# Weight sums ahead of two output DMAs, a router's table from one-hots in parts, and the choices' weights on GpSimd: one step of a hybrid decoder layer

## The chip, the core and the metric

One core of a Trainium2 chip runs the whole program: TensorE (matmuls, PE), VectorE (DVE), ScalarE (ACT), GpSimd (POOL) and SyncE (SP, which only issues DMAs here), each with its own queue of instructions, and 16 DMA engines. The metric is the device time of one execution in microseconds (us), the median of several runs. Lower is better.

## What is computed

One decoder layer on 1024 prompt tokens and on 8 sequences of 4 new tokens, 1056 rows in all, of width 1024, in float32. Cut to what matters:

```python
h    = rmsnorm(x, norm_mix)
proj = h @ w_in                          # 1024 -> N_IN columns, split among three token mixers
#  A gated DeltaNet (4 heads x 128, short conv on q/k/v, chunks)
#  B chunked causal spatial gating (4 groups x 64)     C RWKV-7 (4 heads x 64)
x    = x + concat(o_a, o_b, o_c) @ w_out
# hierarchical MoE
h    = rmsnorm(x, norm_ffn)
gsel = argmax(gl)                        # 1 of 4 groups, gl = h @ router_group_w + b
gw   = softmax(gl)[gsel]
top_v, top_i = top_k(el[gsel], 2)        # 2 of the group's 4 experts
tw   = softmax(top_v) * gw               # weights of the two choices
x    = x + sum_e gate[e] * ((silu(h @ w_gate[e]) * (h @ w_up[e])) @ w_down[e])
y    = rmsnorm(x, norm_final)
```

The new recurrent states, the last convolution rows and the last normalised row of each sequence (`shift_prompt`, `shift_sample`) are outputs too.

## The kernel before

All order is written by hand: each engine has one program, and the engines meet through semaphores (`wait_ge`, `then_inc`). A wait holds up all that stands behind it in the same engine's program.

**The projection.** Activations lie transposed in `hT`. The first 14 column blocks of `w_in` (v, the q/k/v blocks of mixer A) are taken two blocks at a time, a *pair*, by a Strassen-like scheme of seven half-size products (`seven_products(p, ch)`, matmuls at L553) in place of eight: for each pair p (0 to 6) and each half of the tokens, ch = 0 or 1, the products M1, M6, M2, M7, M4, M5, M3 follow one another, each eight matmuls and a bit under 1.8 us. M1, M2, M4, M3 and others use four sums and differences of the pair's weight halves, t1 to t4, or the halves themselves. GpSimd makes these sums in `weight_sums(p)` (L463 to L468): four subtractions of 128 x 512, with two drains. It waits for the pair's weights (`w_in`, loaded by SyncE in `load_pair(p)`) and, from p = 2 on, for the last product of pair p-2 (`s.prod`), which frees the buffers of the sums. TensorE waits for `s.sums_w >= p+1` before the first product of a pair. VectorE adds the products into the outputs (`halves`, L1089 to L1100), and does the short convolution of each finished block in between (L1107 to L1119); the products rotate through six PSUM banks, so a product waits for the add of the product six places before it.

GpSimd's program in this stretch is: sums of pair 0, sums of pair 1, a small mask product (L473), then a wait for `s.shc >= 2` and two DMAs with the last normalised rows (L475, L476), then sums of pairs 2 and 3, a wait and a DMA (L480), sums of pairs 4 to 6. `s.shc` counts two copies by VectorE (L1028) of rows that TensorE transposed in `last_tokens(0)` and `last_tokens(1)` (L583); the second of these stands behind all products of pair 1.

**The router's table.** At the end of the output projection each token has two choices c = 0, 1 of an expert. Tokens lie in TILES = 9 tiles of up to 128; each choice gets a place, a *slot* of 32 rows (`sk`) and a row in it (`fl`), by a chain of small steps on VectorE (`step` is one operation and a drain, so all of these steps have line 2786). Then for each choice two one-hots are made: `Arow` (L2870, 18 x 32 elements per partition) of the row, `Bcol` (L2875, 9 x 104 per choice) of the slot. `Arow` times `behind` gives the half of `Aid` that carries row numbers (GpSimd, L2251), `Arow` times the choice's weight `route.w` the half that carries weights (VectorE, L2874). 18 matmuls (L2534) of `Aid` by `Bcol`, 9 for each choice, sum up the table; it is turned by one more step (L2537, L2538) into lists of rows and of weights by slot. The five steps that make `route.w` from the exponentials stand in the middle of VectorE's chain, between the first slots of the experts and the ranks:

```python
dve.wait_ge(s.ex, 2)
step(dve.tensor_reduce, den[:], route.exps[:, :, 0:NG], AX_X, ALU.add)
step(dve.scalar_tensor_tensor, den[:], route.exps[:, :, NG], 1.0, den[:], ALU.add, ALU.mult)
step(dve.reciprocal, route.w[:, 0], den[:])
step(dve.tensor_tensor, route.w[:, 1], route.exps[:, :, NG], route.w[:, 0], ALU.mult)
step(dve.tensor_scalar, route.w[:, :, NT], route.w[:, :, NT], route.valid[:], None, ALU.mult)
```

**The experts.** With the table known, GpSimd gathers the rows of a slot by indirect DMAs (L3018), and TensorE works through some 76 slots (L3086, L3097), while SyncE loads the experts' weights. Expert 0's weights are asked for as soon as the output projection is over.

## Time and profile before

| what | value |
|---|---|
| median of 3 runs | 1267.41 us (1266.54 to 1269.93) |
| the profiled execution's own time | 1270.75 us |
| its span in the trace | 1269.0 us |
| TensorE busy (matmuls) | 1188.6 us, 94% |
| VectorE, ScalarE, GpSimd busy | 518.8, 339.5, 560.3 us |
| mean granted TensorE clock | 0.97 |

The trace is of one execution; every number in the rows below is from it, in us from the start of its span unless marked ns. A line number is one of the kernel before. Idle time of an engine costs only where something that ends late waits for that engine, so the rows are to be read for who waited for whom, and in which order.

### The profile page before, as it was taken

Reading aid. Unit: us, or ns where it says so; the run is one execution under the profiler, and the core shown is the slowest. Engines: PE = TensorE matmul, PEld = TensorE weight load, DVE = VectorE, ACT = ScalarE, POOL = GpSimd, SP = SyncE. Lnnn points to the kernel's source line nnn. Section 1 sums busy time; section 2 is a strip of 40 time slices with the busy share of each in tenths; the row PEclk is TensorE's granted clock in tenths of the full one; section 3 lists DMA queues with packets and bytes.
Section 4 is the critical chain, followed back from the end, with each engine's and each line's share of the span. In section 5 each row is a group of like instructions: output and inputs, shape, how many; then the busy total and the mean of one; then the engine's idle time right before and its main releaser. Section 6 shows DMA issues by size and latency. Waiting matters only on the chain. (4 is left out here: it accounts for less than half of the span.)

```text
span 1269.0 us, 31522 instructions
## 1 busy us (share of the span) xinstructions
PE 1188.6 (94%) x12736; PEld 849.9 (67%) x12736; DVE 518.8 (41%) x1252; ACT 339.5 (27%) x787; POOL 560.3 (44%) x818
## 2 busy tenths in 40 slices
PE   9996999999999999999998999959999999999990
PEld 7785888856666667778764554447777777777760
DVE  3453887755285524564532113252222222222223
ACT  5002003253342145456432132211111111111114
POOL 7403111020650236878732021026666666666662
PEclk9998999999999999999998999969999999999995
DMA  6301120114303100000084313189999897898838
GB/s 208 100 1 34 35 67 18 32 60 137 63 21 92 50 17 15 17 23 16 11 243 159 101 67 113 45 303 381 308 373 338 270 374 247 289 374 288 266 51 290
DMA packets 139882, 187.12 MB, mean 147 GB/s; under 512 B 37272, under 2 KB 85903, under 8 KB 139786
## 3 DMA queue, kind: packets, MB, share of 16 engines
q1 hardware_dynamic: 123018, 164.87, 38.3%
q0 software_dynamic: 15936, 20.57, 7.8%
q8 instruction: 69, 1.13, 0.4%
q10 hardware_dynamic: 832, 0.33, 0.1%
q14 instruction: 27, 0.22, 0.1%
HBM read 156.41 MB, written 29.32 MB: 146 GB/s over the span
## 5 line engine op out<-in xcount | busy, mean ns | idle before, releaser
L527 PE MATMUL ps<-hT,w_in 128*128 128x352 f32 (+1 forms) x624 | 190.1, 464 | 1.8 <-ACT cb L806 1.2
L527 PEld LDWEIGHTS ps<-hT,w_in 128*128 128x128 f32 x624 | 118.0, 191 | 69.3 <-issue 4.6
L3041 POOL DMA_INDIRECT sum_rows<-slot_out,scatter_rows x76 | 121.9, 1604 | 38.2 <-POOL scatter_rows L3040 25.7
L3173 DVE TENSOR_TENSOR slot_T<-slot_raw_T,vecs 128x256 f32<-128x256 f32 x75 | 32.5, 434 | 208.5 <-PE ps L3086 207.6
L3086 PE MATMUL ps<-qkv,slot_T 128*32 128x256 f32 x1920 | 109.9, 379 | 3.1 <-DVE slot_T L3173 1.6
L3086 PEld LDWEIGHTS ps<-qkv,slot_T 128*32 128x32 f32 x1920 | 74.8, 110 | 32.3 <-DVE slot_T L3173 4.2
L3018 POOL DMA_INDIRECT gathered<-h_rows,gather_rows x79 | 83.5, 1057 | 19.6 <-issue 12.2
L3130 ACT ACTIVATE slot_silu<-ps 128x128 f32<-128x128 f32 x77 | 21.4, 278 | 225.0 <-PE ps L3086 222.8
L3086 PE MATMUL ps<-cb,slot_T 128*32 128x256 f32 x1408 | 80.6, 379 | 0.0
L3086 PEld LDWEIGHTS ps<-cb,slot_T 128*32 128x32 f32 x1408 | 55.4, 110 | 20.5
L3136 ACT ACTIVATE slot_out<-ps,slot_weights 128x256 f32<-128x256 f32 x76 | 36.2, 476 | 112.2 <-PE ps L3097 112.2
L2260 PE MATMUL ps<-qkv,zg 128*128 128x512 f32 (+1 forms) x128 | 61.3, 623 | 0.0
L3028 POOL COPY gather_rows<-slot_rows 128x1 uint32 (+1 forms) x76 | 56.0, 737 | 6.7 <-DMA gathered<-h_rows,gather_rows 6.1
L3097 PE MATMUL ps<-qkv,slot_hidden_T 128*32 128x256 f32 x960 | 58.1, 379 | 0.8 <-ACT slot_out L3136 0.8
L3181 DVE STREAM_TRANSPOSE slot_hidden_T<-slot_hidden 128x128 f32<-128x128 f32 x74 | 23.1, 313 | 72.6 <-PE ps L3097 72.5
L1118 DVE SCALAR_TENSOR_TENSOR zg<-qkv,vecs,zg 128x1021 f32<-128x1021 f32 (+2 forms) x36 | 49.2, 1367 | 3.0 <-issue 0.4
L3040 POOL COPY scatter_rows<-slot_sums 128x1 uint32 (+1 forms) x76 | 15.6, 206 | 75.8 <-ACT slot_out L3136 75.8
L3097 PEld LDWEIGHTS ps<-qkv,slot_hidden_T 128*32 128x32 f32 x960 | 37.7, 110 | 15.2 <-issue 1.3
L3097 PE MATMUL ps<-third_w_down,slot_hidden_T 128*32 128x256 f32 x704 | 42.6, 379 | 0.0
L3097 PE MATMUL ps<-zg,slot_hidden_T 128*32 128x256 f32 x704 | 42.6, 379 | 0.0
L2260 PEld LDWEIGHTS ps<-qkv,zg 128*128 128x128 f32 (+1 forms) x128 | 22.7, 187 | 28.7 <-issue 28.1
L2658 DVE TENSOR_TENSOR residual<-residual,ps 128x512 f32<-128x512 f32 (+1 forms) x16 | 11.0, 685 | 67.3 <-PE ps L2260 67.3
(748 smaller groups left out, 2405.0 us busy)
## 6 DMA issues: line engine op xcount, KB each, us to landing
qkv<-in_expert_w_gate SPq DMA_DIRECT2D x6, 2048.0 KB
qkv<-in_expert_w_up SPq DMA_DIRECT2D x6, 2048.0 KB
qkv<-in_expert_w_down SPq DMA_DIRECT2D x6, 2048.0 KB
cb<-in_expert_w_gate SPq DMA_DIRECT2D x5, 2048.0 KB
cb<-in_expert_w_up SPq DMA_DIRECT2D x5, 2048.0 KB
zg<-in_expert_w_down SPq DMA_DIRECT2D x5, 2048.0 KB, 21.8
third_w_down<-in_expert_w_down SPq DMA_DIRECT2D x5, 2048.0 KB, 17.0
w_in<-in_w_in SPq DMA_DIRECT2D x18, 512.0 KB, 4.7
```

Of the source, the lines that this page charges most:

```text
L527: last = pe.matmul(pbank(b)[:, c, 0:n], w[:, k, :], hT[:, k, c * CH:c * CH + n], start=(k == 0), stop=(k == KD - 1))
L1118: dve.scalar_tensor_tensor(acc[u][:, d:SEQ], x[:, 0:SEQ - d], wv, acc[u][:, d:SEQ], ALU.mult, ALU.add)
L2260: last = pe.matmul(ps[0:n, half, :], mix[k][:, where(i)], wo[:, k, half * 512:half * 512 + 512], start=(k == 0), stop=(k == KD - 1))
L3018: pool.indirect_dma_start(ring[r][:], None, quarter_rows, bass.IndirectOffsetOnAxis(ap=idx[:, r:r + 1], axis=0)).then_inc(in_ring[r], 16)
L3028: pool.tensor_copy(idx[:, r:r + 1], route.token[:, ds(q + RING, 1)]).then_inc(s.ix, 1)
L3041: pool.indirect_dma_start(quarter_sums, bass.IndirectOffsetOnAxis(ap=sidx[:, r:r + 1], axis=0), y[r][:], None, compute_op=ALU.add).then_in ...
L3086: last = pe.matmul(gu_bank[c4[c], 0:2 * QF].rearrange("p (x b d) -> p x b d", x=2, d=32), xT[:, k, :], of_quarter(by_block[u][k], c), star ...
L3097: last = pe.matmul(y_bank[c4[c], 0:QD], heT[:, c4[k]], wd[u][:, k, c * QD:c * QD + QD], start=(k == 0), stop=(k == 3))
L3130: act.activation(sl[:], gu_bank[:, 0:QF], ACT.Silu).then_inc(s.silu, 1)
L3136: act.activation(y[r][:], y_bank[:, 0:QD], ACT.Copy, scale=route.weight[:, ds(q, 1)]).then_inc(s.acc, 1)
L3173: dve.tensor_tensor(xT[:], xr[:], bc(nf, 2, ROWS_SLOT), ALU.mult).then_inc(s.xT, 1)
L3181: dve.transpose(heT[:], he[:]).then_inc(s.hT, 1)
```

## The change

Three edits.

1. In GpSimd's program `weight_sums(2)` stands ahead of the wait for `s.shc` and its two DMAs; `weight_sums(3)` stays behind them.
2. The choices' weights: VectorE keeps only the reciprocal, without a drain, placed behind the step that gives the slot. GpSimd makes the denominator in four operations once the exponentials are there, and, behind the reciprocal, the second choice's weights and the mask of the tile of sampled rows. The two engines hand over through two counting semaphores, `choice_pool` and `choice_dve`.
3. The product of `Arow` by the second choice's weights goes to GpSimd, as its third product, behind a drain. Each choice's `Bcol` is made in two parts, tiles 0 to 3 and 4 to 8, and TensorE waits for the parts one by one.

```diff
+CHOICE_POOL = {"den": 1, "weights": 2, "id0": 3, "id1": 4, "rw1": 5}
+CHOICE_DVE = {"one_over_den": 1, "row": 2}
+TABLE_PARTS = ((0, 4), (4, 9))
...
                 weight_sums(1)
                 pool.wait_ge(s.samp_w, 16 * NB * H)
                 pool.tensor_tensor(m.sguS[:], m.sguS[:], bc(m.causal4[:], 1, H), ALU.mult).then_inc(s.consts, 1)
+                weight_sums(2)
                 pool.wait_ge(s.shc, 2)
                 pool.dma_start(O["shift_prompt"].rearrange("o b d -> (o b) d"), last_rows[0:1, :]).then_inc(s.shift_out, 16)
                 pool.dma_start(O["shift_sample"].rearrange("o b d -> (o b) d"), last_rows[1:1 + NB, :]).then_inc(s.shift_out, 16)
-                weight_sums(2)
                 weight_sums(3)
...
-                pool.wait_ge(s.row, 1)
+                pool.wait_ge(s.ex, 2)
+                pool.tensor_tensor(den_pairs[:], route.exps[:, :, 0:2], route.exps[:, :, 2:4], ALU.add)
+                pool.tensor_scalar(den_top[:], route.exps[:, :, NG], 1.0, None, ALU.add)
+                pool.drain()
+                pool.tensor_tensor(den[:], den_pairs[:, :, 0], den_pairs[:, :, 1], ALU.add)
+                pool.drain()
+                pool.tensor_tensor(den[:], den[:], den_top[:], ALU.mult).then_inc(s.choice_pool, 1)
+                pool.wait_ge(s.choice_dve, CHOICE_DVE["one_over_den"])
+                pool.tensor_tensor(route.w[:, 1], route.exps[:, :, NG], route.w[:, 0], ALU.mult)
+                pool.drain()
+                pool.tensor_scalar(route.w[:, :, NT], route.w[:, :, NT], route.valid[:], None, ALU.mult).then_inc(s.choice_pool, 1)
+                pool.wait_ge(s.choice_dve, CHOICE_DVE["row"])
                 for c in range(2):
                     of_c = slice(c * TILES, c * TILES + TILES)
-                    pool.tensor_tensor(Aid[:, of_c, 0:ROWS_SLOT], Arow[:, of_c], behind[:], ALU.mult).then_inc(s.id, 1)
+                    pool.tensor_tensor(Aid[:, of_c, 0:ROWS_SLOT], Arow[:, of_c], behind[:], ALU.mult).then_inc(s.choice_pool, 1)
+                pool.drain()
+                pool.tensor_tensor(Aid[:, TILES:2 * TILES, ROWS_SLOT:2 * ROWS_SLOT], Arow[:, TILES:2 * TILES],
+                                   bc(route.w[:, 1], 2, ROWS_SLOT), ALU.mult).then_inc(s.choice_pool, 1)
...
                 for c in range(2):
-                    pe.wait_ge(s.id, c + 1)
-                    pe.wait_ge(s.rw, c + 1)
-                    pe.wait_ge(s.slot, c + 1)
-                    for a in range(c * TILES, c * TILES + TILES):
+                    if c == 0:
+                        pe.wait_ge(s.rw, 1)
+                    pe.wait_ge(s.choice_pool, CHOICE_POOL["id0" if c == 0 else "rw1"])
+                    for t, a in enumerate(range(c * TILES, c * TILES + TILES)):
+                        if t in (0, TABLE_PARTS[1][0]):
+                            pe.wait_ge(s.slot, 2 * c + (1 if t == 0 else 2))
                         last = pe.matmul(table[64 * (a % 2):64 * (a % 2) + 64], Aid[:, a, :], Bcol[:, a, :], start=a < 2, stop=a >= 2 * TILES - 2)
...
-                dve.wait_ge(s.ex, 2)
-                step(dve.tensor_reduce, den[:], route.exps[:, :, 0:NG], AX_X, ALU.add)
-                step(dve.scalar_tensor_tensor, den[:], route.exps[:, :, NG], 1.0, den[:], ALU.add, ALU.mult)
-                step(dve.reciprocal, route.w[:, 0], den[:])
-                step(dve.tensor_tensor, route.w[:, 1], route.exps[:, :, NG], route.w[:, 0], ALU.mult)
-                step(dve.tensor_scalar, route.w[:, :, NT], route.w[:, :, NT], route.valid[:], None, ALU.mult)
                 dve.wait_ge(s.rank, 1)
...
                 step(dve.tensor_scalar, sk[:], fl[:], -ROUND, None, ALU.add)
+                dve.wait_ge(s.choice_pool, CHOICE_POOL["den"])
+                dve.reciprocal(route.w[:, 0], den[:]).then_inc(s.choice_dve, 1)
                 step(dve.scalar_tensor_tensor, fl[:], sk[:], -float(ROWS_SLOT), rk[:], ALU.mult, ALU.add)
...
                 for c in range(2):
                     of_c = slice(c * TILES, c * TILES + TILES)
-                    dve.tensor_tensor(Aid[:, of_c, ROWS_SLOT:2 * ROWS_SLOT], Arow[:, of_c], bc(route.w[:, c], 2, ROWS_SLOT), ALU.mult).then_inc(s.rw, 1)
-                    dve.tensor_tensor(Bcol[:, of_c], bc(iota[:, 0:TABLE], 1, TILES), bc(sk[:, c], 2, TABLE), ALU.is_equal).then_inc(s.slot, 1)
+                    if c == 0:
+                        dve.wait_ge(s.choice_pool, CHOICE_POOL["weights"])
+                        dve.tensor_tensor(Aid[:, of_c, ROWS_SLOT:2 * ROWS_SLOT], Arow[:, of_c], bc(route.w[:, c], 2, ROWS_SLOT), ALU.mult).then_inc(s.rw, 1)
+                    for t0, t1 in TABLE_PARTS:
+                        dve.tensor_tensor(Bcol[:, c * TILES + t0:c * TILES + t1], bc(iota[:, 0:TABLE], 1, t1 - t0), bc(sk[:, c, t0:t1], 2, TABLE),
+                                          ALU.is_equal).then_inc(s.slot, 1)
```

How the instructions stand in the engines' programs. First GpSimd in the projection, from the mask product to the sums of pair 3 (those on `pre` are pair 2's, those on `qkv` pair 3's), before:

```order
L473 TENSOR_TENSOR sgu_wT_sample<-sgu_wT_sample,causal4 32x128 [waits s_samp_w]
L475 DMA out_shift_prompt<-cb 16x1x64 [waits s_shc]
L476 DMA out_shift_sample<-cb 8x1024
L463 TENSOR_TENSOR pre_0<-w_in_1,w_in_0 128x512 [waits s_prod,s_w1,s_w0]
L465 TENSOR_TENSOR pre_0<-w_in_1,pre_0 128x512
L466 TENSOR_TENSOR pre_1<-w_in_1 128x512
L468 TENSOR_TENSOR pre_1<-w_in_0,pre_0 128x512
L463 TENSOR_TENSOR qkv<-qkv 128x512 [waits s_prod,s_w1,s_w0]
```

and with the change:

```order
L476 TENSOR_TENSOR sgu_wT_sample<-sgu_wT_sample,causal4 32x128 [waits s_samp_w]
L466 TENSOR_TENSOR pre_0<-w_in_1,w_in_0 128x512 [waits s_prod,s_w1,s_w0]
L468 TENSOR_TENSOR pre_0<-w_in_1,pre_0 128x512
L469 TENSOR_TENSOR pre_1<-w_in_1 128x512
L471 TENSOR_TENSOR pre_1<-w_in_0,pre_0 128x512
L479 DMA out_shift_prompt<-cb 16x1x64 [waits s_shc]
L480 DMA out_shift_sample<-cb 8x1024
L466 TENSOR_TENSOR qkv<-qkv 128x512 [waits s_prod,s_w1,s_w0]
```

The four operations on pair 2 passed the two DMAs; the wait for `s_shc` now stands between the sums of pairs 2 and 3.

Second, VectorE in the tail of its chain, with the change. (Semaphores of this late stage reuse those of earlier ones and are shown by the earlier names: `s_mix` is `choice_pool`, `s_var` is `choice_dve`, and below `s_vc` is `ex`.)

```order
L2805 TENSOR_TENSOR r_first_slot<-r_incl,r_nslots 128x16
L2805 SCALAR_TENSOR_TENSOR rank<-r_first_slot,ps 128x144 [waits s_ev]
...
L2805 TENSOR_SCALAR r_slot<-r_row 128x18
L2882 RECIPROCAL choice_weights<-r_choice_den 128x9 [waits s_mix]
L2805 SCALAR_TENSOR_TENSOR r_row<-r_slot,r_row_of_all 128x18
L2885 TENSOR_TENSOR ub<-iota_row,r_row 128x576
L2891 TENSOR_TENSOR ub<-ub,choice_weights 128x9x32 [waits s_mix,s_var]
L2893 TENSOR_TENSOR bb<-iota_row,r_slot 128x416
L2893 TENSOR_TENSOR bb<-iota_row,r_slot 128x520
L2893 TENSOR_TENSOR bb<-iota_row,r_slot 128x416
L2893 TENSOR_TENSOR bb<-iota_row,r_slot 128x520
```

The five weight steps between `r_first_slot` and `rank` are gone, one of them is back late in the chain, and of the products by weights one is left.

Third, GpSimd in the same place, with the change; before, only the two operations on `rows_from_spare` stood here.

```order
L2252 TENSOR_TENSOR r_den_pairs<-choice_exps 128x18 [waits s_vc]
L2253 TENSOR_SCALAR r_den_top<-choice_exps 128x9
L2255 TENSOR_TENSOR r_choice_den<-r_den_pairs 128x9
L2257 TENSOR_TENSOR r_choice_den<-r_choice_den,r_den_top 128x9
L2259 TENSOR_TENSOR choice_weights<-choice_exps,choice_weights 128x9 [waits s_var]
L2261 TENSOR_SCALAR choice_weights<-choice_weights,valid_sample_row 128x2
L2265 TENSOR_TENSOR ub<-ub,rows_from_spare 128x9x32 [waits s_var]
L2265 TENSOR_TENSOR ub<-ub,rows_from_spare 128x9x32
L2267 TENSOR_TENSOR ub<-ub,choice_weights 128x9x32
```

Six small operations come ahead of the two large ones, and one more large one behind them.

## Rows read from the trace of the kernel before

**Rows 1.** The page, part 2: busy tenths and granted clock in 40 slices.
```profile
PE   9996999999999999999998999959999999999990
PEclk9998999999999999999998999969999999999995
```
**Rows 2.** Who waited for whom, TensorE: us in total, times, longest.
```profile
PE ps L553 <- POOL pre L468: 10.1, 1, 10.1
```
**Rows 3.** Timeline of TensorE, 107 to 125 us: start, us, what, idle before.
```profile
107.86 0.60 PE L583 MATMUL ps<-ident,hT 128*9 128x128 f32 x4
118.57 3.86 PE L553 MATMUL ps<-hT,w_in 128*128 128x264 f32 x8 [10.11 <-POOL pre L468]
...
124.71 1.94 PE L553 MATMUL ps<-hT,w_in 128*128 128x264 f32 x8
```
**Rows 4.** Timeline of TensorE, 55 to 60 us: the same order, pair 0.
```profile
55.61 0.60 PE L583 MATMUL ps<-ident,hT 128*9 128x128 f32 x4
...
59.61 1.94 PE L553 MATMUL ps<-hT,qkv 128*128 128x264 f32 x8
```
**Rows 5.** Timeline of TensorE, at 82 us: what follows pair 0's last product.
```profile
81.84 1.04 PE L590 MATMUL ps<-ident,vbn 128*128 128x128 f32 x8
```
**Rows 6.** Timeline, GpSimd, 109 to 123 us: shift DMA, first and last sum of pair 3.
```profile
109.47 0.54 POOL L475 DMA_DIRECT2D out_shift_prompt<-cb  x1 [52.80 <-DVE cb L1028]
...
118.27 1.26 POOL L463 TENSOR_TENSOR qkv<-qkv 128x512 f32<-128x512 f32 x1
...
122.31 1.27 POOL L468 TENSOR_TENSOR qkv<-qkv 128x512 f32<-128x512 f32 x1
```
**Rows 7.** Windows: PE, PEld, DVE, ACT, POOL busy; granted clock, DMA share, GB/s.
```profile
60.00:62.00 2.00, 2.00 (x10) 1.71 (x10) 0.66 (x2) 0.00 (x0) 0.00 (x0) 1.00 0.22 55
...
108.50:118.50 10.00, 0.00 (x0) 0.00 (x0) 0.67 (x2) 0.00 (x0) 6.30 (x7) 0.74 0.42 109
...
113.00:114.00 1.00, 0.00 (x0) 0.00 (x0) 0.00 (x0) 0.00 (x0) 0.00 (x0) 0.70 0.12 25
```
**Rows 8.** Timeline, VectorE around two convolutions, and TensorE's M2 behind the first.
```profile
127.34 0.17 DVE L1108 COPY conv_tails<-qkv 128x24 f32<-128x24 f32 x1
...
133.01 0.43 DVE L1093 TENSOR_TENSOR qkv<-qkv,ps 128x264 f32<-128x264 f32 x1
...
137.17 1.94 PE L553 MATMUL ps<-hT,w_in 128*128 128x264 f32 x8
...
154.37 1.25 DVE L1108 COPY conv_tails<-qkv 128x24 f32<-128x24 f32 x1
...
163.04 0.43 DVE L1093 TENSOR_TENSOR qkv<-qkv,ps 128x264 f32<-128x264 f32 x1
```
**Rows 9.** The table: timeline rows; the others by line, with ns min/median/max.
```profile
830.91 0.19 DVE L2786 TENSOR_REDUCE r_choice_den<-choice_exps 128x9 f32<-128x36 f32 x1
...
832.27 0.30 DVE L2786 SCALAR_TENSOR_TENSOR rank<-r_first_slot,ps 128x144 f32<-128x144 f32 x1
...
834.73 0.76 DVE L2870 TENSOR_TENSOR ub<-iota_row,r_row 128x576 f32<-128x576 f32 x1
...
L2874 DVE TENSOR_TENSOR ub<-ub,choice_weights x2: 457/750/1043, 835.5 to 837.5; 128x288 f32<-128x288 f32 x2
...
L2875 DVE TENSOR_TENSOR bb<-iota_row,r_slot x2: 1121/1422/1723, 835.9 to 838.5; 128x936 f32<-128x936 f32 x2
...
L2251 POOL TENSOR_TENSOR ub<-ub,rows_from_spare x2: 1062/1370/1677, 835.6 to 836.6; 128x288 f32<-128x288 f32 x2
...
837.77 3.97 PE L2534 MATMUL ps<-bb,ub 128*64 128x104 f32 x36 [7.28 <-DVE bb L2875]
```
**Rows 10.** The first gather and its use; landing times of the gathers, 840 to 875.
```profile
844.60 1.11 POOL L3018 DMA_INDIRECT gathered<-h_rows,gather_rows  x1 [6.33 <-POOLq L2150]
...
849.45 0.19 POOL L3028 COPY gather_rows<-slot_rows 128x1 uint32<-128x1 uint32 x1 [2.46 <-DMA gathered<-h_rows,gather_rows]
...
DMA to landing us min/median/max: 5.8/6.7/7.6
```

More of the change, by code:

```diff
@@ L2038 @@
 o y on ysc yn oT bon yT sout tokm vm sc dS Sup dz zadd zdec zo zof st_out w x0 x1 wr wrn out x2 h2 h2p hT hTd h2o0 h2o1 lp lpc lg lgd rs chosen tot rank
-exd ex row rw slot id table once""".split()
+exd ex choice_dve rw slot choice_pool table once""".split()
 def sample_views(g):
@@ L2108, in output_stage @@
         Aid = g.ub[:].rearrange("p a n -> p (a n)")[:, 2 * TILES * ROWS_SLOT:6 * TILES * ROWS_SLOT].rearrange("p (a n) -> p a n", n=2 * ROWS_SLOT)
-        den = T.sb("r_choice_den", P, TILES)
+        den, den_pairs, den_top = T.sb("r_choice_den", P, TILES), T.sb("r_den_pairs", P, TILES, 2), T.sb("r_den_top", P, TILES)
         Arow, Bcol = row_choice_views(g)
@@ L2867, in _ @@
                 step(dve.tensor_scalar, sk[:], fl[:], -ROUND, None, ALU.add)
+                dve.wait_ge(s.choice_pool, CHOICE_POOL["den"])
+                dve.reciprocal(route.w[:, 0], den[:]).then_inc(s.choice_dve, 1)
                 step(dve.scalar_tensor_tensor, fl[:], sk[:], -float(ROWS_SLOT), rk[:], ALU.mult, ALU.add)
                 pairs = lambda a: a.rearrange("p c t -> p (c t)")
-                dve.tensor_tensor(Arow, bc(iota[:, 0:ROWS_SLOT], 1, 2 * TILES), bc(pairs(fl[:]), 2, ROWS_SLOT), ALU.is_equal).then_inc(s.row, 1)
-                dve.wait_ge(s.row, 1)
+                dve.tensor_tensor(Arow, bc(iota[:, 0:ROWS_SLOT], 1, 2 * TILES), bc(pairs(fl[:]), 2, ROWS_SLOT), ALU.is_equal).then_inc(s.choice_dve, 1)
+                dve.wait_ge(s.choice_dve, CHOICE_DVE["row"])
                 for c in range(2):
                     of_c = slice(c * TILES, c * TILES + TILES)
-                    dve.tensor_tensor(Aid[:, of_c, ROWS_SLOT:2 * ROWS_SLOT], Arow[:, of_c], bc(route.w[:, c], 2, ROWS_SLOT), ALU.mult).then_inc(s.rw, 1)
-                    dve.tensor_tensor(Bcol[:, of_c], bc(iota[:, 0:TABLE], 1, TILES), bc(sk[:, c], 2, TABLE), ALU.is_equal).then_inc(s.slot, 1)
+                    if c == 0:
[4 more added lines that the diff above has]
+                                          ALU.is_equal).then_inc(s.slot, 1)
                 dve.memset(route.first[:, 0:1], 0)
```

## The prediction

> **What bounds the kernel now.** I read the page's 40 slices first. TensorE is busy in nine tenths or more of nearly every slice; the first dip behind the start is the fourth slice, 95 to 127 us, where its granted clock is lower too, and a deeper one is the 27th, 825 to 856 us [rows 1]. So I want the reasons for these two. The list of who waited for whom puts one TensorE wait far ahead of the rest: 10.1 us in the seven-product matmuls of line 553, released by GpSimd's weight sums [rows 2]. TensorE in order of time shows it: four transposes from 107.86, then nothing until 118.57, then products (M1, M6, M2, ...) that run slowly at first, and M2 of the chunk begins at 124.71 [rows 3]. In the window of the pause the granted clock averages 0.74 [rows 7], so the pause also costs clock.
>
> GpSimd is not overloaded there. It sits for 52.8 us in front of an output DMA (line 475), which waits for a small copy that VectorE can only make after TensorE's transposes at 107.86; the sums of pair 2 stand behind that DMA in program order [rows 6]. What the sums themselves need is there much earlier: the products of pair 0 are over when the transposes of line 590 begin, at 81.84 [rows 5], and pair 2's weights stop moving by 62 [rows 7]. The wait is one of order, not of work.
>
> The second dip is the routing table. VectorE walks a chain of small dependent steps, five of them (830.91 to 832.27) for the choices' weights, then builds the one-hots; TensorE, 7.3 us idle, starts the table's matmuls at 837.77 when the last operand of choice 0 is ready [rows 9]. Behind the table come the gathers of the first slot [rows 10], and then the expert stage, in which TensorE is full again.
>
> **Part 1, the weight sums of pair 2 moved ahead of the two shift DMAs.** The same four operations run, and none is added. They may start at 81.84. A set without a long drain takes from 118.27 to 122.31 + 1.27, 5.3 us [rows 6]; so they are done near 87 to 90, 18 us before TensorE asks. The DMAs keep their release (VectorE's copy, behind line 583), so they go out at the same 109.5. Past them only this set moves; pair 3's set is behind them as before, and cannot start before its weights are in, which stop moving in 113 to 114 [rows 7]. That puts its end near 119; TensorE needs it 25 us after the start of pair 2's products, near 134. The output of the sampled rows' values, which GpSimd issues next, and the load of pair 4 on SyncE both hang on TensorE's progress and move with it.
>
> What the wait costs now: at the earlier place with the same order (line 583, M1, M6, M2), M2 begins 59.61 − 55.61 = 4.00 us behind the transposes [rows 4]. Without the pause it would begin here at 107.86 + 4.00 = 111.86. It begins at 124.71 [rows 3]. So **12.85 us** go: the 10.1 of waiting and some 2.7 of matmuls at the lower clock. Neither VectorE nor ScalarE used the pause to catch up (VectorE waited for TensorE right before it), and TensorE has no gap near this size behind it until the tail, so whatever hangs on its progress moves by the same amount.
>
> What can eat into it is VectorE, beside which the sums of pair 3 now run, where before both stood in the pause. VectorE does pair 2's convolution between the add that ends before 127.34 and the add at 133.01: 5.67 us. The same piece for pair 3, beside GpSimd's sums of pair 4, took from 154.37 to 163.04, 8.67 us, so a set of sums costs it **3.0 us** [rows 8]. TensorE needs the result of that add (133.01 + 0.43) when it starts M2 of the next chunk at 137.17 [rows 8]: 3.7 us of slack, unchanged if all moves together. 3.0 is below 3.7, so I cost this at nothing; it is a thin cover, and the bound is below, in rival B. The set for pair 2 itself now runs from 82 on, beside adds without a convolution between them.
>
> **Part 2, the weights' chain on GpSimd.** VectorE loses the five steps: 832.27 − 830.91 = 1.36 us [rows 9]. It gets one reciprocal back without a drain behind it; small operations without a drain start some 0.1 us apart. So the row one-hot (line 2870) begins 1.26 earlier, and ends at 834.73 + 0.76 − 1.26 = 834.23. GpSimd's four operations of the denominator can start with the exponentials, which are there by 830.91, where VectorE uses them now; the reciprocal comes two small steps ahead of the row one-hot at 833.47, near 833. At 0.2 to 0.3 us each they are in time by a microsecond. Its next two wait for the reciprocal and reach choice 0's product 0 to 0.3 us late; I take 0.3, since the second of them will find the row one-hot running.
>
> **Part 3, one-hots in parts and a third product on GpSimd.** Here the rows warn. The two identical VectorE operations of line 2874 took 457 and 1043 ns, those of line 2875 1121 and 1723, GpSimd's of line 2251 1062 and 1677 [rows 9]. The excess is 0.59, 0.60 and 0.62 whatever the size: it looks like waiting out one operation of the other engine, not like a shared rate. So I let the two engines take turns, with 0.46 for a VectorE product, 1.12 × 416/936 = 0.50 and 0.62 for the parts of a column one-hot, and 0.7 for a GpSimd product (the shorter one, 1.06, less the part of VectorE's it overlaps). From 834.5: GpSimd's first, VectorE's product, GpSimd's second, first part of choice 0 (done 836.9), GpSimd's third (837.6), second part (838.2), both parts of choice 1 (839.3). TensorE's 18 tiles take 3.97 us, 0.22 each [rows 9]: four from 836.95, five from 838.3, nine from 839.4, the last ends at 841.4. Now it ends at 837.77 + 3.97 = 841.74. **Gain 0.4 us.** The best case is TensorE starting at once behind the first part, 834.23 + 0.46 + 0.50 + 0.1 = 835.3, and never waiting: end 839.3, gain 2.4. The worst is a late weight that holds choice 0: I allow a loss of 0.5.
>
> Not all of it need arrive. The first gather is issued at 844.60 and its rows are used at 849.45, 4.85 us, with expert 0's weights still moving for the first half; gathers issued in full traffic take 5.8 to 7.6 [rows 10]. Earlier by 0.4, it meets more of that traffic: I count **0.3**.
>
> **Sum.** 12.85 + 0 + 0.3 = 13.15. The profiled execution took 1270.75 us (span 1269.0), so its like would take 1257.6. The median of the three runs, 1267.41, lies 3.3 below the profiled one; against it the forecast is **1254.3**.
>
> **Rivals.**
> **B, VectorE falls behind.** The sums of pair 3 delay VectorE by more than its 3.7 us of slack, and the lag is carried into the sums of pair 4. At most all four GpSimd operations are waited out, 4 × 1.27 = 5.1: a TensorE pause of 1.4, and as much again one pair later. Time 1255.7 to 1257.1, say 1256.4. For it: [rows 8] show 3.0 lost already beside one set. Against it: no TensorE wait there now.
> The Trainium skill, "SBUF — State Buffer", section "SBUF: two separate sides", says that GpSimd and a VectorE operation with two SBUF inputs hold a shared port pair exclusively, for a whole instruction. It speaks against this change at both places; this case's trace agrees at the table (0.59 to 0.62 of excess at three sizes), and by the rule the convolution's steps could all be held, which is B's upper price.
> **C, the table gains in full.** The turns fall kindly, and the gather follows at once: 2.4 in place of 0.3, 1252.2.
> **D, the pause only moves.** Something else that TensorE needs at 108.3 is not there, or pair 3's sums are ready only near 147, and 9.5 us or more come back: about 1265. The wait at 118.57 is on several semaphores, and the trace names only the last. Against it: weights in by 62, and 15 us between the sums of pair 3 and their use.
> **E, slower: the clock.** The pause is a rest for TensorE. If an unbroken run from 40 to 256 us drew the half clock for a stretch, each us of work in it would cost one more. It decides from 13.15 + 3.8 = 17 us of such work on; at 20 the time is 1274. Against it: the clock row stays at 9 through the twelve slices behind the second dip, 380 us of the expert stage with TensorE at 9 in all of them [rows 1].
>
> **How the numbers follow.** Below 0.3%, 3.8 us, a measurement of this kernel can hardly be told from no change. Forecast 0.73 (its own range 1252.8 to 1255.8), B 0.14, C 0.07, D 0.04, E 0.02. All but D and E are faster by over 0.3%: 0.94, same 0.04, slower 0.02. The range reaches from C less about 1 us of scatter between medians (three runs lie 3.4 apart) to above B: 1251.3 to 1258.0.
>
> **What would show it.** Right: in the changed trace GpSimd's four operations on pair 2 lie between 82 and 90 with the shift DMAs still at 109 to 110; the 10.1 us wait is gone, M2 begins near 111.9, the granted clock is 1.00 from 40 to 250; TensorE stays without a wait until the half-product stage ends, everything behind it 12 to 13 us earlier; in the tail, VectorE's rank step follows the first-slot step directly, the GpSimd and VectorE operations show long and short times in turn, and the table's matmuls end 10.4 us behind the start of the step that follows the first-slot step, in place of 10.8 (841.74 − 830.91). Wrong: a new wait of line 553 on VectorE near 120 to 125 (B), a wait of line 553 elsewhere (D), a clock below 1.00 in 108 to 256 (E), or a table that ends 1 to 2 us sooner with the first gather landing as much earlier (C).

## The result, and the profile after

Seven runs of the changed kernel gave a median of **1258.15 us** (1256.99 to 1260.26), seven of the kernel before beside them 1269.93 (1266.54 to 1274.96): a ratio of 0.9908, 95% interval 0.9891 to 0.9924, so 11.8 us less (9.7 to 13.8). The same kernel in a later series, with 17 runs of the kernel before at 1268.02, gave 1258.33 and a ratio of 0.992 (0.9902 to 0.9939): 9.7 us. (One run of the kernel before in a later series, 1309.65 us, was in the chip's slower state and is left out of every mean below.) Faster by over 0.3% was right; the time lies 3.9 us above the forecast of 1254.3 and 0.15 above the end of the range. The profiled execution took 1258.15 us, span 1256.4, against 1269.0 before.

The page of the changed kernel, its 40 slices, against [rows 1]: the dip of the fourth slice is gone in both rows, the one at slices 26 and 27 is not.
```profile
PE   9999999999999999999999999869999999999990
PEclk9999999999999989999999999979999999999995
```
Timeline of TensorE (start, us, what), against [rows 3]: the transposes, then products without a pause. M2 starts at 112.92, 4.00 behind the transposes, in place of 16.85 before.
```profile
108.92 0.60 PE L586 MATMUL ps<-ident,hT 128*9 128x128 f32 x4
109.35 1.95 PE L556 MATMUL ps<-hT,w_in 128*128 128x264 f32 x8
111.14 1.94 PE L556 MATMUL ps<-bb,pre 128*128 128x264 f32 x8
112.92 1.94 PE L556 MATMUL ps<-hT,w_in 128*128 128x264 f32 x8
```
Timeline of GpSimd, against [rows 6]: first and last sum of pair 2 at 83 to 88, the shift DMA where it was, then pair 3's four sums, two of them (1.75 and 2.24) longer than the 1.27 us they take alone.
```profile
83.24 1.27 POOL L466 TENSOR_TENSOR pre<-w_in 128x512 f32<-128x512 f32 x1 [27.21 <-PE ps L556]
...
87.30 1.27 POOL L471 TENSOR_TENSOR pre<-w_in,pre 128x512 f32<-128x512 f32 x1
110.53 0.54 POOL L479 DMA_DIRECT2D out_shift_prompt<-cb  x1 [21.96 <-DVE cb L1031]
...
115.02 1.26 POOL L466 TENSOR_TENSOR qkv<-qkv 128x512 f32<-128x512 f32 x1 [3.40 <-issue]
116.60 1.75 POOL L468 TENSOR_TENSOR qkv<-qkv 128x512 f32<-128x512 f32 x1 [0.32 <-issue]
118.32 2.24 POOL L469 TENSOR_TENSOR qkv<-qkv 128x512 f32<-128x512 f32 x1
```
VectorE beside them, against [rows 8]. From the copy of line 1111 (1108 before) to the next add it now takes 124.82 − 116.22 = 8.60 us (5.67 before). The copy ahead of it, of 3 columns, takes 0.83, 0.66 more than the copy of 24 columns in [rows 8], two of the three long steps take 2.13 and 2.36 in place of 1.28, and the short one between them 1.25 in place of 0.25. The last row is TensorE's M2 of the next chunk, which uses the add of 124.82.
```profile
115.48 0.83 DVE L1110 COPY conv_tails<-qkv 128x3 f32<-128x3 f32 x1
116.22 0.16 DVE L1111 COPY conv_tails<-qkv 128x24 f32<-128x24 f32 x1
...
117.30 2.13 DVE L1121 SCALAR_TENSOR_TENSOR zg<-qkv,vecs,zg 128x1021 f32<-128x1021 f32 x1
119.36 1.25 DVE L1122 SCALAR_TENSOR_TENSOR zg<-pre,vecs,zg 128x32 f32<-128x32 f32 x1
120.69 2.36 DVE L1121 SCALAR_TENSOR_TENSOR zg<-qkv,vecs,zg 128x1022 f32<-128x1022 f32 x1
...
124.82 0.43 DVE L1096 TENSOR_TENSOR qkv<-qkv,ps 128x264 f32<-128x264 f32 x1
...
125.38 1.98 PE L556 MATMUL ps<-hT,w_in 128*128 128x264 f32 x8
```
The add ends at 125.25, 0.13 before TensorE asks: the cover held at this place, with nothing left of it. (The M2 group lasts 1.98 in place of 1.94.)

VectorE's lag of 3.6 us is then carried on, and it meets TensorE 39 us later. TensorE's small products of the sampled rows (line 607, 604 before) need VectorE's product of line 1081 (1078 before). Behind M2 of pair 2, VectorE starts the last of these at 50.57 us in place of 49.49. Before, it was done 0.4 us ahead of TensorE; now TensorE waits 0.69 us. The rows of the changed kernel:
```profile
163.49 0.69 DVE L1081 TENSOR_TENSOR ub<-ub,cb 128x512 f32<-128x512 f32 x1
...
164.32 0.42 PE L607 MATMUL ps<-sgu_wT_sample,cb 32*64 32x32 f32 x8 [0.69 <-DVE ub L1081]
```
And of the kernel before:
```profile
174.20 0.69 DVE L1078 TENSOR_TENSOR ub<-ub,cb 128x512 f32<-128x512 f32 x1
...
175.27 0.42 PE L604 MATMUL ps<-sgu_wT_sample,cb 32*64 32x32 f32 x8
```
From M2 to the end of the last product of pair 6 TensorE takes 132.48 us before and 133.33 with the change.

The table, against [rows 9]. The three engines in order of time: the denominator's last operation, the step behind the first-slot step, the reciprocal, the two operations of the weights around the row one-hot, the first product, the column one-hots, and the table's matmuls.
```profile
818.29 0.24 POOL L2257 TENSOR_TENSOR r_choice_den<-r_choice_den,r_den_top 128x9 f32<-128x9 f32 x1
...
818.81 0.30 DVE L2805 SCALAR_TENSOR_TENSOR rank<-r_first_slot,ps 128x144 f32<-128x144 f32 x1
...
821.01 0.22 DVE L2882 RECIPROCAL choice_weights<-r_choice_den 128x9 f32<-128x9 f32 x1
...
821.31 0.20 POOL L2259 TENSOR_TENSOR choice_weights<-choice_exps,choice_weights 128x9 f32<-128x9 f32 x1 [2.77 <-DVE choice_weights L2882]
821.34 0.79 DVE L2885 TENSOR_TENSOR ub<-iota_row,r_row 128x576 f32<-128x576 f32 x1
821.69 0.60 POOL L2261 TENSOR_SCALAR choice_weights<-choice_weights,valid_sample_row 128x2 f32<-128x2 f32 x1 [0.17 <-issue]
...
822.39 0.97 DVE L2891 TENSOR_TENSOR ub<-ub,choice_weights 128x288 f32<-128x288 f32 x1 [0.27 <-POOL choice_weights L2261]
823.28 3.37 DVE L2893 TENSOR_TENSOR bb<-iota_row,r_slot 128x416 f32<-128x416 f32 x4
...
824.60 3.69 PE L2553 MATMUL ps<-bb,ub 128*64 128x104 f32 x36 [6.22 <-DVE bb L2893]
```
The table ends at 828.29, 9.48 behind the step of 818.81 (10.83 before). The first gather (GpSimd's timeline, against [rows 10]) is issued 831.17 − 818.81 = 12.36 behind that step, 1.33 sooner than before (844.60 − 830.91 = 13.69); but its rows are used 18.62 behind it, where it was 18.54.
```profile
831.17 1.12 POOL L3037 DMA_INDIRECT gathered<-h_rows,gather_rows  x1 [6.18 <-POOLq L2153]
...
837.43 0.19 POOL L3047 COPY gather_rows<-slot_rows 128x1 uint32<-128x1 uint32 x1 [3.88 <-DMA gathered<-h_rows,gather_rows]
```
The two profiled executions cut at the same four events (the third gate and up product is where the slots begin to follow each other without a gap):

| us | before | after |
|---|---|---|
| start to the transposes | 107.86 | 108.92 |
| to M2 of pair 2 | 16.85 | 4.00 |
| to the step behind the first-slot step | 706.20 | 705.89 |
| to the third gate and up product | 30.62 | 30.42 |
| to the end | 407.5 | 407.2 |

The gain of the spans stands in the second row, and 1.1 of it is given back in the first, which ends before anything that the change moves. The third row hides a loss: the 0.85 us that TensorE lost up to the end of pair 6 are in it, and are made up by a loop around 300 us in which TensorE stops longer in this execution of the kernel before (5.52 against 4.51 us for the loop; see "The start" below).

### The profile page after: what moved, and what is told of

Read it like the earlier page. It is cut to its first block and busy times, and to the rows that moved or that the text cites. A ratio compares the mean times of both kernels' runs of the same rounds, so it can differ in the third digit from the quotient of the medians.

```text
span 1256.4 us, 31526 instructions
## 1 busy us (share of the span) xinstructions
PE 1187.0 (94%) x12736; PEld 848.4 (68%) x12736; DVE 520.4 (41%) x1249; ACT 338.6 (27%) x787; POOL 562.9 (45%) x825
## 5 line engine op out<-in xcount | busy, mean ns | idle before, releaser
L530 PE MATMUL ps<-hT,w_in 128*128 128x352 f32 (+1 forms) x624 | 192.7, 468 | 1.8 <-ACT cb L809 1.2
L3037 POOL DMA_INDIRECT gathered<-h_rows,gather_rows x79 | 83.5, 1057 | 19.5 <-issue 12.2
```

Of the source, the lines that this page charges most:

```text
L530: last = pe.matmul(pbank(b)[:, c, 0:n], w[:, k, :], hT[:, k, c * CH:c * CH + n], start=(k == 0), stop=(k == KD - 1))
L3037: pool.indirect_dma_start(ring[r][:], None, quarter_rows, bass.IndirectOffsetOnAxis(ap=idx[:, r:r + 1], axis=0)).then_inc(in_ring[r], 16)
```

## The experiments

In the trace the gain is part 1's, less the 0.85 us behind it, and parts 2 and 3 gain 1.3 us that vanish. The theory: part 1 alone makes the time, and the table's gain dies in the first gather. Rivals: the table has its share; the clock, or VectorE, takes part of the gain.

**Each part alone.** e1, the kernel before with the one line moved:
```diff
+                weight_sums(2)
                 pool.wait_ge(s.shc, 2)
...
-                weight_sums(2)
                 weight_sums(3)
```


> Only the sums of pair 2 are moved ahead of the shift DMAs; the table is as before. Theory (the pause is nearly all of the change, the table's gain is lost at the first gather): 12.8 us less than before, within 0.5 us of the whole change. Rival 1 (the table brings its 1.3 us through to the end, the moved sums bring less): 10.5 to 11.5 us less. Rival 2 (the table part costs time at the end): 13.5 or more less.


Measured: 1258.11 us (1255.92 to 1260.19), ratio 0.9905 (0.9886 to 0.9925). It is the whole change's time, and its trace has the new wait too (0.84 us, line 604 on VectorE's line 1078), so that wait belongs to part 1.

e2, the changed kernel with this edit undone:


> Only the table's part of the change; the sums of pair 2 stand behind the shift DMAs as before, with the 10 us pause. Theory: the table's matmuls end 1.3 us sooner behind the rank step, the first gather is issued 1.3 us sooner and its rows are used no sooner, so the time is within 0.5 us of before. Rival 1: 1.3 us less than before. Rival 2: 0.5 to 1.5 us more than before.


Measured: 1269.16 us (1265.46 to 1273.45), ratio 0.9992 (0.9977 to 1.0006). The wait is back (10.33 us), the table ends 9.48 behind the step as in the changed kernel, and the time doesn't show it. By the interval alone parts 2 and 3 could be worth 2.9 us or cost 0.8. The traces are sharper: in all eleven profiles of kernels with the weight loads as before, the first gather's rows are used 18.50 to 18.64 us behind the step, five with the old table and six with the new one. So the table's gain ends there, and nothing of it is left behind the first gather.

**Where the table's gain goes.** In the changed kernel expert 0's weights are still moving when the first gather is issued. Windows of its trace (columns as in [rows 7]; the last two are DMA share and GB/s):
```profile
834.00:835.00 1.00, 1.00 (x10) 1.00 (x9) 0.00 (x0) 0.00 (x0) 0.00 (x0) 0.86 1.04 414
835.00:836.00 1.00, 1.00 (x12) 1.00 (x11) 0.00 (x0) 0.00 (x0) 0.00 (x0) 1.00 0.70 254
836.00:837.00 1.00, 0.35 (x4) 0.15 (x2) 0.00 (x0) 0.00 (x0) 0.00 (x0) 1.00 0.06 12
```
Before, they thin out 12 us later (414 GB/s in 846 to 847, 66 in 848 to 849). In both kernels the rows are used some 1.8 us behind that, not so long behind the issue. e3 asks for expert 0's down projection only when the first gather has landed:
```diff
 # SyncE, end of the output stage
                 sp.wait_ge(s.st_out, 16 * 3 * H)
-                load_down(sp, A, wd[0], 0, moe_sems.d0)
...
                 sp.wait_ge(in_ring[0], 16)
+                load_down(sp, A, wd[0], 0, in_d[0])
                 load(1)
```


> The whole change, and the down projection of expert 0 (2 MB) is asked for only when the first gather has landed. Theory (the first gather's landing is set by expert 0's weight traffic): the weights' first part stops some 5 us sooner, the gather lands 4 to 5 us behind its issue instead of 6.3, its rows are used 1.5 to 3 us sooner, and the time falls by 1 to 3 us against the changed kernel, unless the down projection or the next gathers come late by as much. Rival (the landing is a fixed latency of the gather): no gain, or a loss of up to 3 us, since the down projection comes late.


Measured: 1256.04 us (1255.62 to 1257.39), 2.1 below the changed kernel and below e1, which ran beside it. Its gather is issued at the same time and is back 3.97 us later, not 6.26:
```profile
831.11 1.12 POOL L3037 DMA_INDIRECT gathered<-h_rows,gather_rows  x1 [6.18 <-POOLq L2153]
...
835.08 0.19 POOL L3047 COPY gather_rows<-slot_rows 128x1 uint32<-128x1 uint32 x1 [1.59 <-DMA gathered<-h_rows,gather_rows]
```
This is shown: what bounded that place was the weight traffic, and the table's gain was covered by it. In the five profiles with the late load the rows are used 15.34 to 16.32 behind the step.

e6, the same with expert 1's weights held behind the third gather (`sp.wait_ge(in_ring[2], 16)` ahead of `load(1)`):


> The kernel of e3_down_late, and expert 1's weights are asked for only when the third gather (the first to be issued behind the first use) has landed. If that gather too is held by weight traffic, it lands in 4 to 5 us in place of 6.4, TensorE's third slot starts up to 2 us sooner, and the time falls by 0.5 to 2 us against e3. If expert 1's weights then come late at TensorE (their 6 MB need some 16 us, from about 840), the time rises instead, by up to 3 us.


Measured: 1255.18 us (1252.46 to 1256.47), 0.9 below e3, with overlapping runs; e11 below comes back to it.

**VectorE's slack.** e4 makes the sums of pair 3 twice in the changed kernel (a loop around its four subtractions):


> The whole change, with the sums of pair 3 made twice over (same values). Theory (VectorE has no slack left beside these sums, its add comes in at TensorE's start of M2 to within 0.1 us): a second set costs VectorE's convolution another 2 to 4 us and TensorE now waits that much in line 556 at M2 of the second half of pair 2; time 1.5 to 4 us above the changed kernel. Rival (turn-taking is small beside what VectorE has to spare): no TensorE wait, no change in time. The sums themselves then end near 128, 8 us before TensorE needs them, so they are not the wait.


Measured: 1263.93 us (1260.56 to 1265.36), 5.8 above the changed kernel. The timeline of TensorE is rival B as the prediction drew it, with twice its price: a wait of 3.14 us, and behind it matmuls of 3.88 and 2.97 us in place of 1.94.
```profile
127.06 3.88 PE L560 MATMUL ps<-hT,w_in 128*128 128x264 f32 x8 [3.14 <-DVE qkv L1100]
130.74 2.97 PE L560 MATMUL ps<-zg,pre 128*128 128x264 f32 x8
133.55 1.94 PE L560 MATMUL ps<-hT,pre 128*128 128x264 f32 x8
```
From the transposes to the M4 group it takes 133.55 − 107.30 = 26.25 us, 6.2 more than in the changed kernel (128.97 − 108.92). A wait of 3.1 us cost as much again in clock: from 127 to 131 us the granted clock is 0.50. (TensorE now comes late enough to line 607 that its wait there is gone, and at the end of pair 6 the loss is 5.1 to 5.4 us.)

**The clock's share of the pause.** e5, the kernel before with 36 matmuls of `ident` in the pause:
```diff
                 last_tokens(1)
+                pe.wait_ge(s.vc, 3)
+                for k in range(36):
+                    pe.matmul(ps[:, 6, 0:P], m.ident[:], m.ident[:], start=True, stop=True)
```


> The kernel before, with 36 idle matmuls of 128 columns on TensorE in the pause, into a bank that nobody reads. Theory (2.7 of the 12.85 us are clock): the granted clock stays at 1.00 over the pause, the products behind it take 1.8 us each at once, and the time falls by 2 to 2.7 us. Rival (the slow products are something else, a start-up of matmuls behind a wait): they stay slow, no change.


Measured: 1270.33 us (1265.48 to 1271.98), ratio 1.0007 (0.9992 to 1.0021). Inconclusive by its time: the matmuls ended at 116.4, a wait of 2.29 us was left, and the clock fell after it instead of in it (windows: granted clock third from the end of each row).
```profile
108.50:118.50 10.00, 7.88 (x71) 7.68 (x69) 0.55 (x1) 0.00 (x0) 6.20 (x7) 1.00 0.43 110
118.50:125.00 6.50, 6.33 (x21) 5.16 (x22) 0.43 (x1) 1.67 (x2) 4.89 (x4) 0.74 0.00 0
```
M2 began 16.25 us behind the transposes, against 16.85. The same stretch takes 16.81, 15.94 and 17.25 in e2, e9 and e13, which have the pause as it was, so these 0.6 us are within what executions differ by, and the 2.7 stay the prediction's reading of the rows.

**The start.** In the profiles of the changed kernel, e1 and e3 the group at 35.5 us takes 20.86 (20.82 in e3) where it takes 19.17 in the others of that time, its clock at 0.50 for 2 us. e7 is e3 with this:
```diff
+                for k in range(6):
+                    pe.matmul(ps[:, 2, 0:P], m.ident[:], m.ident[:], start=True, stop=True)
                 pe.wait_ge(s.hT, TILES)
                 pe.wait_ge(s.hT, TILES + 1)
                 chunk("v0", 2).then_inc(s.pj, 1)
```


> The kernel of e3_down_late with six idle matmuls of 128 columns ahead of the last wait of the start, where TensorE has only very small matmuls and an idle 0.6 us, and where three of six profiled runs show half clock from 36 us on (1.7 us lost). If the small matmuls are what lets the clock fall, the median falls by 0.5 to 1 us and the runs lie closer together; if not, it rises by up to 0.3 us.


Measured: 1251.42 us (1249.76 to 1253.1), 4.6 below e3: much more than expected. e8 is the changed kernel again, beside e5 to e7:


> The changed kernel again, unedited, on the chip of these runs: to compare e3, e6 and e7 with. 1258 us, as e1 within 0.5 us, and 2 us above e3.


Measured: 1258.33 us (1256.94 to 1259.24).

e9 and e10 put the six matmuls alone into the kernel before and into the changed one, e11 joins e6 and e7:


> The kernel before, with six matmuls of 128 columns into an unused part of bank 2 ahead of TensorE's wait for the last tiles of hT at 34.8 us, and nothing else. Theory: in the profiles of the change, of the sums-only run and of the late-down run TensorE's clock fell to 0.5 for about 3 us after its short waits at 34 to 36 us and the next stage took 1.7 us longer; this is a matter of the single execution, and the kernel before has it as often as the change. Then this kernel is 1 to 4 us below the kernel before, as much as the same edit takes off the changed kernel. Rival: the kernel before has no such fall (its profile shows none), and the measured gain of the change was cut short because the change has it: then this kernel is within 0.8 us of the kernel before, and the edit takes 3 us or more off the changed kernel.


Measured: 1267.73 us (1264.56 to 1268.69; the kernel before beside it 1268.44).


> The changed kernel with the same six matmuls ahead of the wait at 34.8 us. Theory (a matter of the execution, alike in both): 1 to 4 us below the changed kernel's 1258.2, and the distance to the same edit on the kernel before stays at 10 to 11 us. Rival (the change alone suffers from the fall): 3 us or more below 1258.2, and the distance between the two kernels with this edit grows to 12.5 to 13.5 us, which is what the prediction had.


Measured: 1255.3 us (1254.57 to 1256.97). 2.9 to 3.0 below the changed kernel, and 12.4 below e9.


> The change, expert 0's down projection asked for behind the first gather, expert 1's weights behind the third gather, and the six matmuls at the start together. Theory: the parts add up: 1251.4 of the busy start with the late down projection, less the 0.9 us that the late expert 1 was worth: 1250.5, range 1249.0 to 1252.0. Rival: the late expert 1 was worth nothing and its 0.9 us was scatter: 1251.4, and the slot stage begins no sooner behind the rank step than the 27.4 us of that run.


Measured: 1252.78 us (1251.91 to 1253.41), no better than e7: the rival holds, and no gain of the late expert 1 shows.

The start alone can't give 3 to 4.6 us, since only 1.7 (20.86 − 19.17) are lost there. What else was different stood in the list of TensorE's waits, in the rows without a releaser. Of the kernel before:
```profile
PE ps L733 <- issue: 2.4, 1, 2.4
```
Of the changed kernel:
```profile
PE ps L736 <- issue: 1.9, 1, 1.9
```
These are one stop each, amid 256 small matmuls of the same line that follow each other every 9 ns (2.36 us for all); here in the timeline of the changed kernel, behind the 156th:
```profile
293.49 1.53 PE L736 MATMUL ps<-qkv 128*32 128x32 f32 x156
296.94 1.06 PE L736 MATMUL ps<-qkv 128*32 128x32 f32 x100 [1.92 <-issue]
```
In e10 the same loop (now line 738) runs through:
```profile
292.71 2.36 PE L738 MATMUL ps<-qkv 128*32 128x32 f32 x256
```
In e5, with 36 matmuls more ahead of it, the stop is there, but 56 small matmuls further on, behind the 212th:
```profile
307.63 0.86 PE L736 MATMUL ps<-qkv 128*32 128x32 f32 x44 [2.04 <-issue]
```
Six matmuls that end at 36.5 us can't change the data of a loop at 293; they do change where its instructions stand in TensorE's stream. Two theories, then: the busy start, or the place in the stream. e12, e13 and e14 have six matmuls too, of 32 by 32, with next to no work, in the changed kernel, the kernel before and e3:
```diff
+                for k in range(6):
+                    pe.matmul(ps[0:32, 2, 0:32], m.ident[0:32, 0:32], m.ident[0:32, 0:32], start=True, stop=True)
```


> The changed kernel with six matmuls of 32 by 32 at the place where the busy start has six of 128 by 128: as many instructions ahead of everything that follows, but next to no work in the wait at 34.8 us. In the profiles so far TensorE stops for 1.8 to 2.4 us in the middle of the 256 small matmuls of line 736 (156 of them done), waiting for nothing the profile shows, and its clock is below 1.00 right behind; in all four profiles with the six large matmuls that stop is gone. Theory (the place in TensorE's instruction stream decides): the stop at line 736 is gone here too, and the median is 1.5 to 3.0 us below the changed kernel's 1258.2, so near 1255.3. Rival (keeping TensorE busy at 34.8 us decides): the stop is there with 1.8 us or more, and the median is within 0.8 us of 1258.2.


Measured: 1255.15 us (1253.81 to 1255.57): the time of e10, 1255.3.


> The kernel before with the same six small matmuls. Theory (the place in the stream decides, and its price is paid in both kernels): the stop at line 733 is gone, and the median is 0.5 to 3 us below the kernel before; the difference to the changed kernel with the same edit is 12 to 13 us. Rival (the busy start decides): the stop stays and the median is that of the kernel before within 0.8 us.


Measured: 1267.35 us (1265.41 to 1269.78; the kernel before beside it 1268.41): 1.1 less, and 12.2 above e12.


> The change with expert 0's down projection asked for behind the first gather, and the six small matmuls. Theory (place in the stream): as fast as with the six large ones, 1251.4, within 1 us. Rival (busy start): 1256.0, as without them, within 1 us.


Measured: 1251.98 us (1251.71 to 1252.57), within 0.6 of e7.

The stop is gone in all three, so the place in the stream decides, and keeping TensorE busy at 34.8 us is worth nothing that these runs can tell. e13 also settles the start: it computes in the order of the kernel before and has the slow group, which the kernel before, e2 and e5 lack, while e8, e4, e6 and e12 with the new order lack it. So it is not tied to the change; it comes in some executions (5 of the 16 profiled) and not in others. The timeline of e13:
```profile
35.72 20.86 PE L527 MATMUL ps<-hT,w_in 128*128 128x352 f32 x64
```
The loop takes 4.43 to 5.52 us in the nine profiles with the stop and 2.36 in all seven without it, so the stop costs 2.1 to 3.2 us, and no less with the old order of GpSimd's program (2.5 to 3.2) than with the new one (2.1 to 2.4).

The trace names no releaser, but the list of DMA queues has one named "instruction" whose packets are of 16 KB. In all nine profiles with the stop (windows of 0.2 us) one such packet starts 0.9 to 1.6 us into the loop, and TensorE goes on 2.4 to 3.0 us behind its start. In all seven without it the packet starts 1.9 to 2.2 us ahead of the loop. In the changed kernel, window 294.4 to 294.6 (packets, MB, share of 16 engines):
```profile
q8 instruction: 1, 0.02, 29.5%
```
In e10, window 290.6 to 290.8, where the loop begins at 292.71:
```profile
q8 instruction: 1, 0.02, 38.0%
```
That TensorE stops because its next instructions have not arrived fits all sixteen profiles; that the packet is TensorE's is not shown.

**The best version** of these is the changed kernel with the late down projection and six matmuls more: e7 1251.42 us, ratio 0.9863 (0.9841 to 0.9884), and e14 1251.98, 0.9867 (0.9848 to 0.9887). By their medians that is 6.2 to 6.7 us below the changed kernel.

## Why the prediction was nearly right, and where it failed

- **The wait (12.85 us): right.** M2 begins 4.00 us behind the transposes, to the hundredth what [rows 4] gave, and the clock is 1.00 in 108.5 to 118.5. e1 has the whole gain. The 12.85 are one execution's: in four profiles with the pause as it was, M2 comes 15.94 to 17.25 us behind the transposes, so the pause costs 11.9 to 13.3.
- **The step that failed: VectorE, "I cost this at nothing". It cost about 1 us.** At the place that the prediction looked at, the cover held. The slack was 3.7 and 3.6 of it went: 2.93 between the rows of 116.22 and 124.82, and 0.66 in the copy ahead (e4 shows the price where it doesn't suffice: twice the wait). But the slack spent there was missing later. TensorE waits 0.64 to 0.84 us for VectorE at line 607 (604 in e1) in all ten profiles with the new order, e4 left out, and never there in the five with the old one. From M2 to the end of pair 6 it takes 133.33 to 133.63 us in those ten and 132.48 to 132.49 in those five: 0.85 to 1.15 us of the 12.85 are given back. "TensorE stays without a wait until the half-product stage ends" was wrong. This is rival B's mechanism, a lag carried on, at less than its price of 1.4 to 2.8.
- **What a set of sums costs VectorE: 3.0 was no fixed price.** The prediction took it from a later pair. Here a set took 3.6, and pair 4's, later, took 0.97 where it had taken 3.0 (the two steps of line 1081 at 142.43 and 144.45 lasted 1.34 and 1.01 in place of 0.69). With that, and without a pause of 0.57 that VectorE made before, only 1.1 of the lag was left at the wait. The Trainium skill, "SBUF — State Buffer", section "SBUF: two separate sides", has a GpSimd operation that reads SBUF and a VectorE operation with two SBUF inputs exclude each other for a whole instruction. The rows of 117.30, 119.36 and 120.69 agree: they grew by 0.85, 1.00 and 1.08, each by less than one GpSimd operation of 1.27, and together by the 2.93. The copy of 115.48, with one input, lasted 0.83 for 0.17 and ended at 116.31, as GpSimd's sum of 115.02 did (116.28); whether it waited for that pair of ports no run here shows.
- **Part 2: right.** The weights' chain came 0.27 us late for choice 0, and its second operation took 0.60 beside the row one-hot, as drawn.
- **Part 3: mis-sized, by 0.5 to 0.9 us, in a place that doesn't count.** The table gained 1.35 against the kernel before, not 0.4 (0.9 against e1 and e5, whose old table ends 10.39 and 10.41 behind the step in place of 10.83). TensorE began at 824.60, 5.8 behind the step; the strict turns I had drawn were too slow for the four parts of the column one-hots, which took 3.37 together.
- **"I count 0.3" of the first gather: wrong, it was 0.** I let a gather issued earlier gain three quarters of it; its landing hung on the end of expert 0's traffic, which the prediction had in view. The eleven profiles under e2, and e3, show it. Rival C fell with it: its first half happened and its second did not.
- **Rivals D and E: did not happen.** No wait of D's size came back, and the granted clock is 1.00 from 40 to 250 us.
- **The sum.** With VectorE's loss of about 1 us and nothing for the gather, 13.15 becomes some 11.8. Measured, the two kernels lie 9.7 to 11.8 us apart by medians, and 12.2 (e12, e13) and 12.4 (e9, e10) with the stop gone. What the prediction passed over in the list of waits, the stop of 2.4 us, is no part of this: both kernels have it. By medians its removal is worth 3.0 us to the changed kernel and only 0.7 to 1.1 to the kernel before, but a median serves badly there: 27 of 79 runs of the kernel before took 1270 us or more, and none of the 24 of e9 and e13. By means the removal is worth 2.2 and 2.4 us to the kernel before (e9, e13) and 2.9 to 3.4 to the changed one, and the kernels lie 10.2 to 11.7 apart with the stop (this result, e1, e8) and 12.0 to 12.4 without. The rest is of the size by which series of runs differ, and no run here takes it apart.
- **The base.** Medians of more runs of the kernel before are 1268.0 to 1269.9, where the three on record gave 1267.41. This would have set the forecast higher by 0.6 to 2.5. In the series of the result, with 1269.93, the base makes 2.5 of the 3.9 us, and the other 1.3 are what VectorE and the gather make; in that of e8, with 1268.02, the base makes 0.6 of 4.0. That the first sum comes out so well is luck.

## What to carry to other kernels

A transfer or a wait that an in-order engine reaches early holds everything behind it: ask at every long idle time whether the work behind the wait was ready, and move it ahead. When what moves makes another engine late, the slack that this uses up at the first meeting is missing at the next ones: follow that engine until it has caught up, and cost each wait on the way. Before speeding up what leads to a transfer, look at whether the transfer's landing follows its issue or the end of other traffic; if it is the traffic, moving a load is worth more than making the table faster. And read the waits without a releaser: a stop in the middle of many equal instructions may hang on where they stand in the stream, so an experiment that adds a few instructions needs a control that adds as many without the work.

## What was not expected of the hardware

- Six matmuls of 32 by 32 at 35 us took away a stop of 1.8 to 2.4 us some 260 us later, and the medians fell by 3.0 us (changed kernel) and 4.1 (e3). That the stop is TensorE waiting for instructions to arrive is an inference, from the packets of the instruction queue.
- A stop of TensorE costs more than its length: 3.1 us of waiting came to 6.2 (e4), and the group at 35.5 us, behind waits of 0.6 us, took 20.86 in place of 19.17 in some executions and not in others. Windows of the changed kernel there:
```profile
36.00:38.00 2.00, 2.00 (x5) 1.02 (x4) 2.00 (x2) 0.00 (x0) 0.00 (x0) 0.50 0.91 204
38.00:40.00 2.00, 2.00 (x7) 1.28 (x6) 2.00 (x1) 0.00 (x0) 0.00 (x0) 0.76 1.09 301
```
And of the kernel before, at the full clock:
```profile
36.00:38.00 2.00, 1.84 (x6) 1.25 (x7) 1.91 (x2) 0.00 (x0) 0.00 (x0) 1.00 0.57 115
```
- The first gather took 6.26 us from issue to use beside 254 to 418 GB/s of weight traffic, and 3.97 without it (2.98 to 3.97 in the five kernels with the late load).
